# First token gather of the expert stage: its index column, and which engine makes the three low parts ahead of it

## The reference

```python
affinity = jax.nn.softmax((xt @ w_router).astype(jnp.float32), axis=-1)
gates, idx = lax.top_k(affinity.T, cap)          # cap: 64 of the sample rows, 32 of the prompt rows
def one_expert(args):
    ids, g, wg, wu, wd = args
    xe = xt[ids]
    hdn = jax.nn.silu(xe @ wg) * (xe @ wu)
    return (hdn @ wd) * g[:, None].astype(x.dtype)
ye = lax.map(one_expert, (idx, gates, w_gate, w_up, w_down))
out = jnp.zeros_like(xt).at[idx.reshape(-1)].add(ye.reshape(-1, D))
```

## Time and profile before

| | us |
|---|---|
| median of 3 runs | 2149.92 (2148.94 to 2152.68) |
| the profiled execution, its own time | 2150.25 |
| its span in the profile | 2148.4 |
| PE busy | 2051.1 (95%) |
| DVE busy | 1657.8 (77%) |
| ACT busy | 1294.5 (60%) |
| POOL busy | 190.9 (9%) |
| mean granted TensorE clock | 0.981 of full |

### The profile page before, as it was taken

One profiled execution on the slowest core, in us unless ns is written; L12 is line 12 of the kernel. 1 busy time (PEld: TensorE's weight loads), 2 busy tenths in 40 slices (PEclk: granted clock), 3 DMA queues, 4 the chain that ended last, 5 costly groups with the idle time before them and its releaser, 6 DMA issues.

```text
span 2148.4 us, 27211 instructions
## 1 busy us (share of the span) xinstructions
PE 2051.1 (95%) x9878; PEld 1491.6 (69%) x9878; DVE 1657.8 (77%) x1346; ACT 1294.5 (60%) x1131; POOL 190.9 (9%) x118
## 2 busy tenths in 40 slices
PE   6999898999859999999999999999999999999996
PEld 5766667578737777777777777777777777777775
DVE  4533947573548888888888888888888888888887
ACT  4213212452247777777777777777777777777775
POOL 1000312110030101010110101011010101101000
PEclk9999999998979999999999999999999999999999
DMA  7225213404469999999999999999999999999994
GB/s 198 93 103 186 89 51 106 176 11 186 153 217 370 362 383 368 383 369 381 374 370 384 365 384 369 382 373 370 385 366 384 368 383 374 370 384 367 385 366 184
DMA packets 310264, 637.60 MB, mean 297 GB/s; under 512 B 19272, under 2 KB 83144, under 8 KB 308682
## 3 DMA queue, kind: packets, MB, share of 16 engines
q1 hardware_dynamic: 306506, 624.00, 80.0%
q0 software_dynamic: 3712, 12.98, 2.5%
HBM read 610.20 MB, written 26.74 MB: 296 GB/s over the span
## 4 chain that ended last, share of the span: by engine, by line
PE 88%; DVE 6%; issue 2%; ACT 2%; DMA 2%; POOL 0%; SPq 0%; POOLq 0%; ACTq 0%; DVEq 0%
PE bank L922 22%; PE bank L920 22%; PE bank L921 22%; PE bank L647 5%; PE bank L854 3%; PE bank L727 3%; PE bank L781 2%; PE bank L658 2%; PE bank L737 2%; PE bank L959 1%; DVE ysum_sample L1414 1%; PE bank L756 1%; PE bank L768 1%; DVE ysum_prompt L1414 1%; DVE uspec L1414 1%
## 5 line engine op out<-in xcount | busy, mean ns | idle before, releaser
L1666 DVE TENSOR_TENSOR split_ring<-breg,split_ring 128x2048 fp32r<-128x2048 f32 x525 | 1202.2, 2290 | 198.0 <-ACT split_ring L1230 198.0
L1230 ACT CAST split_ring<-breg 128x2048 fp32r<-128x2048 f32 x525 | 1004.3, 1913 | 398.7 <-PE bank L922 398.7
L920 PE MATMUL bank<-split_ring,xe_split 128*96 128x512 f32 (+1 forms) x1536 | 582.8, 379 | 1.6 <-DVE xe_split L1677 1.6
L922 PE MATMUL bank<-split_ring,xe_split 128*96 128x512 f32 (+1 forms) x1536 | 578.7, 377 | 0.0
L921 PE MATMUL bank<-split_ring,xe_split 128*96 128x512 f32 (+1 forms) x1536 | 574.7, 374 | 0.0
L922 PEld LDWEIGHTS bank<-split_ring,xe_split 128*96 128x96 f32 x1536 | 248.3, 162 | 90.4
L921 PEld LDWEIGHTS bank<-split_ring,xe_split 128*96 128x96 f32 x1536 | 249.3, 162 | 85.8
L920 PEld LDWEIGHTS bank<-split_ring,xe_split 128*96 128x96 f32 x1536 | 248.7, 162 | 85.3 <-DVE xe_split L1677 1.9
L920 PE MATMUL bank<-split_ring,ht_split 128*96 128x512 f32 x704 | 277.9, 395 | 1.7 <-DVE ht_split L1684 1.5
L922 PE MATMUL bank<-split_ring,ht_split 128*96 128x512 f32 x704 | 276.9, 393 | 0.0
L921 PE MATMUL bank<-split_ring,ht_split 128*96 128x512 f32 x704 | 276.2, 392 | 0.0
(11 more groups left out here) (217 smaller groups left out, 1699.6 us busy)
## 6 DMA issues: line engine op xcount, KB each, us to landing
breg<-in_w_down SPq DMA_DIRECT2D x176, 1024.0 KB, 7.1
breg<-in_w_up SPq DMA_DIRECT2D x175, 1024.0 KB, 7.2
breg<-in_w_gate SPq DMA_DIRECT2D x174, 1024.0 KB, 6.5
w_raw<-in_w_in SPq DMA_DIRECT2D x24, 512.0 KB, 4.2
filter_spectra<-kf_out SPq DMA_DIRECT2D x6, 1024.0 KB, 5.6
kf<-filter_spectra SPq DMA_DIRECT2D x6, 1024.0 KB, 6.9
w_out_raw<-in_w_out SPq DMA_DIRECT2D x4, 1024.0 KB, 8.9
bias<-in_attn_bias SPq DMA_DIRECT2D x8, 448.0 KB, 5.6
```

What stands on the lines that cost most here:

```text
L920: pe.matmul(out, x_hi, w_hi, start=start, stop=False)
L922: return pe.matmul(out, x_lo, w_hi, start=False, stop=stop)
L1230: act.copy(sp_unit[n % SPLIT_RING][0], raw[slot]).then_inc(hi_done, 1)
L1666: dve.tensor_tensor(sp_unit[s][1], raw[later_place(n, e)[0]], sp_unit[s][0].bitcast(F32), ALU.subtract).then_inc(lo_done, 1)
```

## The change

POOL makes the low part of unit 0 alone. DVE makes those of units 1 and 2, after `chosen_done` and before `tokens_lo(1)`. POOL then issues the first gather straight from column 0 of `idxT` when `chosen_done` has come; the copy into `idx_gather` is gone, and `pool_step` is raised by 2 as before, so later counts stand.

```diff
+            dve.wait_ge(lo_done, 1)
+            for n in range(1, SPLIT_RING):
+                lo_part(n, 0)
             tokens_lo(1)
...
-            for n in range(SPLIT_RING):
-                pool.wait_ge(hi_done, n + 1)
-                if n == SPLIT_RING - 1:
-                    pool.wait_ge(logit_mm, TILES)
-                pool.tensor_tensor(sp_unit[n][1], raw[raw_place(n)[0]], sp_unit[n][0].bitcast(F32),
-                                   ALU.subtract).then_inc(lo_done, 1)
+            pool.wait_ge(hi_done, 1)
+            pool.tensor_tensor(sp_unit[0][1], raw[raw_place(0)[0]], sp_unit[0][0].bitcast(F32),
+                               ALU.subtract).then_inc(lo_done, 1)
...
-            def gather(index_set, count):
+            def gather(index_set, count, index):
                 pool.wait_ge(xn_out, 32 * TILES)
                 pool.wait_ge(index_set, count)
-                pool.indirect_dma_start(xg, None, xn_dram, bass.IndirectOffsetOnAxis(ap=idx_gather, axis=0),
+                pool.indirect_dma_start(xg, None, xn_dram, bass.IndirectOffsetOnAxis(ap=index, axis=0),
                                         bounds_check=last_row).then_inc(gathered, 16)
...
-            pool.wait_ge(chosen_done, 1)
-            pool.tensor_copy(idx_gather, idxT[:, 0:1]).then_inc(pool_step, 2)
-            gather(pool_step, 2)
+            gather(chosen_done, 1, idxT[:, 0:1])
+            pool.sem_inc(pool_step, 2)
...
-                gather(pool_step, e * 2 + 4)
+                gather(pool_step, e * 2 + 4, idx_gather)
```

## The result

Over 20 runs of each kernel the changed one took 2148.69 us in the median (2143.83 to 2151.85), the kernel before 2151.84 (2148.94 to 2154.6). The ratio is 0.9984 with a 95% interval of 0.9978 to 0.9991: 3.4 us less, between 1.9 and 4.7. The prediction said 2144.4 (2141.3 to 2148.3), so the time lies 0.4 us above the range. Of the 4.3 us between forecast and median, 1.9 are the old kernel's own: over 20 runs its median is that much higher than over the three that the forecast started from. The other 2.4 are the gain: the forecast lay 5.5 under its median of before, and the two medians now lie 3.15 apart.

The account below looks back on a forecast made before the run. The prediction took PE's dependence chain from the first multiplication, held by the late gather, as the bound. Landing at 609.4 instead of 615.12 saves 5.7 us, giving 2144.4 us against 2149.92, range 2141.3 to 2148.3.

Parts of the forecast that it names:

- What bounds the kernel: PE sets the pace; one dependence chain starts at 618.29, with 8.2 us between a ready index and the gather.
- D: Rival: expert loop settles in another rhythm and gets slower; at 1 us more per period 2158.5 us; chance 0.04.
- E: Rival: something else holds unit 0 until 618, so the change moves nothing; time 2149.9 us; chance 0.04.
- Start of the operation: POOL's gather operation starts about 0.85 us after the index table is ready, at 603.4.
- Two low parts on DVE: Units 1 and 2's low parts take 2.29 us each in DVE's idle time before the landing, hidden.
- POOL passes after the first low part: Gather's operation gets in between DVE's two low parts at 604.8 and ends 0.88 us later, at 605.7.
- rival A: DVE keeps POOL out through both low parts; operation ends at 608.0, gain 3.9 us, time 2146.2; chance 0.2.
- The flight: Gather's packets queue behind the preload, then need 2.6 us from first packet to landing, at 609.4.
- rival C: Gather isn't held up, or its packets share engines with the preload; gain 7.4 us, time 2142.7; chance 0.1.
- The sum: Start of unit 0 moves from 618.29 to 612.6, 5.7 us sooner, and everything behind it moves along.
- The clock: PE's clock is full 4.6 us behind unit 0's start, as before; a 2 us shift would be worth 1 us.
- The page's rule: Skill infers tensor_tensor doesn't hold up descriptor generation, ending the operation at 604.5; prediction held the trace disagrees, 605.7.

Follow-up runs that it names:

- e7: Kernel before, with the gather issued straight from the index table, without the copy; POOL keeps all three low parts. Gather starts 0.18 us behind them; run time not given.
- e3: Changed kernel, with DVE's two low parts each cut into four back-to-back 128x512 operations; gather's operation took 4.98 us, run time not given.
- e13: Changed kernel, with POOL copying the index column again ahead of the gather; that copy took 4.29 us, run time not given.
- e14: Changed kernel, DVE's low parts in four pieces each, plus an unused POOL subtraction ahead of the gather; it ended 1.13 us behind DVE's last piece; run time not given.
- e15: Changed kernel, with DVE's second low part waiting for its first; gather's operation took 2.37 us, run time not given.
- e16: Changed kernel, with POOL's index copy restored and DVE's second low part waiting for its first; the copy took 2.09 us, run time not given.
- e2: Changed kernel, with an unused copy from PSUM between DVE's two low parts; gather's operation took 2.37 us, run time not given.
- e1: Changed kernel, with DVE's two low parts held back until POOL has done the gather's operation; 0.9985 of the kernel before.
- e6: Changed kernel, with a PSUM copy between DVE's low parts and 42, 12 and 22 unused PE transposes in the pauses; run time not given.
- e12: Changed kernel run once more, unaltered, for another profile; run time not given.
- e8: Changed kernel, with DVE's low parts held until the gather's operation is done and the final gain's load moved behind the expert loop; flight 4.6 us, run time not given.
- e11: Kernel before run once more, unaltered, for another profile; run time not given.
- e9: Kernel before, with 45, 12 and 22 unused PE transposes in the pauses around the hand-over; 0.9985 of the kernel before.
- e4: Changed kernel, with 55, 12 and 22 unused PE transposes in the pauses around the hand-over; 0.9970 of the kernel before.
- e5: Kernel before, with 85, 12 and 22 unused PE transposes in the pauses, the first running past the landing; 0.9999 of the kernel before.

## Why the prediction was right and wrong, point by point

*What bounds the kernel.* Right. The chain from POOL's low parts by copy, gather and turn-in to unit 0 held the start, PE's work behind it moved as a whole, and the period stayed at 94.26. Rivals D and E are out.

*Start of the operation.* Right: 0.89 us behind T0 for 0.85, and e7 shows its other part, 0.87 us for the copy and its hand-over.

*Two low parts on DVE.* Right: 4.47 us together (forecast as 2 x 2.29), ended 4.3 us ahead of the landing (605.69 and 609.95). Hidden.

*"POOL passes after the first low part".* This is the step that failed, and rival A, given 0.2, took its place: the operation lasted 4.57 and ended 1.05 us behind the second low part (A had said 0.88 behind). It rested on rows 6 and 7, which were read rightly, but which turned out not to hold for the low parts. The changed kernel, e3, e13 and e14 show that DVE's low parts, back to back, keep a gather, a copy and a subtraction of POOL out; e15 and e16 that a wait of the second for the first lets it in. The forecast's 2.3 us (603.4 to 605.7) is what e2 and e15 have where POOL does pass, 2.37 in both. What sets rows 6 apart, where POOL passed with no pause of DVE's, no run shows, nor why a pause lets it in.

*The flight.* The size was fair by another way. The forecast let the gather queue behind the preload's loads and then gave it the 2.6 us that it takes with idle engines from its first packet to the landing; in e1 its packets run beside the preload's and take 4.9 us (606.99 to 611.84). That they share the engines was in rival C, but it brings no gain. The changed kernel's landing came 3.2 us behind the operation, as A had it (3.17). Had POOL passed, the term would have been about right too: T0 + 6.73 and 6.78 in e2 and e15, for a forecast 609.4 - 602.52 = T0 + 6.9. But at 8.27 in e6 it was not, and e1 shows that a sooner operation hardly helps. Rival C's 7.4 us, which took an idle flight of 3.17, were out of reach for that reason: e1, its case, gains 18.54 - 12.93 = 5.6 us counted from C, and 3.4 from P.

*The sum.* A alone would give 3.9 us, where the forecast had 5.7. Between the two profiled executions unit 0 moved by 5.18 us: 1.23 of these lie ahead of P (596.33 and 595.10) and are no gain of the change, 3.95 are P + 21.96 against P + 18.01. That is A's 3.9. The sum took T0 - P for a constant of this kernel, though, from one execution. Where C - P is 5.7, as in e12, the gain is 22.0 - 19.34 = 2.7. Eight of the 18 executions had C - P of up to 4.2, where 4.0 is won; for the ten others, with a mean of 5.5, it is 22.0 - 5.5 - 13.6 = 2.9. The mean over all, (8 x 4.0 + 10 x 2.9) / 18 = 3.4 us, is what was measured. This is an estimate from 18 executions of mostly other kernels, with a match that may be luckier than it deserves; the measured interval is 1.9 to 4.7. By it, 1.8 of the 2.3 us between the forecast's gain and the measured one are the step that failed, and 0.5 the changing C - P.

*The clock.* The forecast gave it 1 us of spread for its delay behind unit 0; it was 4.6 and 5.8 us. That it can fall a second time at the 3 us pause was not foreseen and cost this profiled execution 2.5 us. It fell for 6.8 us in the changed kernel and in e7, for 3.4 in e1, e3, e12, e13 and e14, and not at all in before, e2, e8, e11, e15 and e16; with the transposes it never fell there (in e6 it was at half from 612.05 to 615.46, around the start of unit 0). That is one of three traces with the old order and six of ten with the new, too few to tell. e7 has the old order of low parts and fell as far as the changed kernel, so the change isn't needed for it. That the change makes it no likelier is supported by the pair e9 and e4, where the gain with the clock held (3.2) is near that without (3.4); but the intervals of the two reach 1.9 and 2.5 us to either side, so that only a large effect is excluded, and the rest stays open.

*The page's rule.* The Trainium skill ("SBUF — State Buffer", "Who interferes with whom") infers that a `tensor_tensor` doesn't hold up descriptor generation. The gather's operation as a whole was held up, and more than rows 4 had shown: 1.18 us alone, 4.57 behind two of them, 4.98 behind eight shorter ones. This doesn't refute the inference as plainly as the prediction said, though: the operation also reads its index column from SBUF, and no run tells that reading from the writing of the descriptors.

## What to carry to other kernels

Before moving work to an engine that idles, look at what the engine that you free will do meanwhile: an operation of GpSimd that starts beside back-to-back SBUF operations of VectorE can be held until the last of them is done, as it was beside the low parts here, though not beside the products at 219 us. Where GpSimd has something urgent, put an operation there that reads PSUM, or a wait of VectorE for the end of the operation ahead (0.12 us here), and look at the timeline to see whether it helped. Then ask what comes next: in e1 the operation came 3.4 us sooner and the rows only 0.7.

One row of a trace, however rightly read, is no proof that two engines share well elsewhere, if types, operations or waits differ: the cheap test is the same pair of operations at the place in question. And when a change moves the start of a chain from one event to another, the gain is the distance of the two events: read it from several executions.

## What the runs showed that had not been expected

VectorE can be kept out by GpSimd too. Its small cast L1652 (16x32, from SBUF to SBUF) takes 0.17 us in e1 and in e12, but lasted until POOL's low part was done where one was under way. The rounds of maxima beside the same low part weren't delayed (0.42 us for each L1611 beside it and after it in e12). In the kernel before:

```profile
599.75 1.12 DVE L1652 CAST idxf<-idxu 16x32 f32<-16x32 uint32 x1
```

It ends at 600.87, POOL's part (596.33 + 4.51) at 600.84. In e5 POOL had its second low part under way:

```profile
603.42 3.87 DVE L1659 CAST idxf<-idxu 16x32 f32<-16x32 uint32 x1
```

Here the index table itself was 3.7 us late (T0 - C of 5.52 for 1.81), and in e9 3.6. The kernel before hides this behind its low parts, which the gather waits for anyway; the changed kernel, with one low part on POOL, can't lose more than what is left of that one.

PE's clock made differences of 114.85 to 120.28 us over one and the same stretch of work, more than the change under study. Transposes in its pauses, which compute nothing, brought the changed kernel from 0.9984 [0.9978, 0.9991] to 0.9970 [0.9959, 0.9982] of the kernel before; the intervals overlap a little.
